# A hybrid diffusion step on one core: the large weight matrices in slabs of one 16 KB run per partition

## The reference, cut to what matters

```
mod = silu(c) @ w_mod[l] + b_mod[l]                 # 1024 x 6144, six blocks of 1024 columns
h   = rms(x, norm1_g) * (1 + sc1) + sh1
u   = h @ w_in[l]                                   # 1024 x 2048, split among four mixers
m   = concat(gqa, pooling, conv, diff attention) @ w_out[l]     # 1024 x 1024
x   = x + g1 * m
h2  = rms(x, norm2_g) * (1 + sc2) + sh2
aff = softmax(h2 @ router_w)                        # 16 experts
gate, idx = top_k(aff.T, 2 * n // 16)               # an expert takes 64 latent and 16 context rows
hid = silu(xe @ wg[e]) * (xe @ wu[e])               # xe = h2[idx], three matrices of 1024 x 1024
x   = x + g2 * scatter_add(idx, hid @ wd[e] * gate)
```

## Time and profile before

| | |
|---|---|
| median of three runs | 2182.03 us |
| profiled execution | 2185.27 us, of which the span of the trace is 2183.4 us |
| mean granted TensorE clock | 0.921 of full speed |
| PE busy | 1843.7 us (84%) |
| PE weight load busy | 1504.9 us (69%) |
| DVE, ACT, POOL busy | 26%, 23%, 17% |
| DMA | 536.37 MB in 145094 packets, mean 246 GB/s |
| ring loads | 228 of 2 MB, by SP's queue (q1) |

### The profile page before, as it was taken

One profiled execution on the slowest core, in us unless ns is written; L12 is line 12 of the kernel. 1 busy time (PEld: TensorE's weight loads), 2 busy tenths in 40 slices (PEclk: granted clock), 3 DMA queues, 4 the chain that ended last, 5 costly groups with the idle time before them and its releaser, 6 DMA issues.

```text
span 2183.4 us, 66044 instructions
## 1 busy us (share of the span) xinstructions
PE 1843.7 (84%) x29563; PEld 1504.9 (69%) x29563; DVE 557.7 (26%) x1095; ACT 506.9 (23%) x1256; POOL 363.2 (17%) x345
## 2 busy tenths in 40 slices
PE   2799998893899998899849999979838998999894
PEld 1455787452898888898725558854538988888883
DVE  0240677234010111101113237742231111011111
ACT  0111554111222121221212125522212212212121
POOL 0130766000000000000002235620000000000001
PEclk8899998995999999999969999979869999999997
DMA  9400300832799999999980040037239999999995
GB/s 349 160 0 8 155 1 1 338 119 105 250 395 387 395 395 391 394 396 393 398 299 13 0 161 2 1 139 263 107 109 370 387 391 398 391 395 395 389 395 192
DMA packets 145094, 536.37 MB, mean 246 GB/s; under 512 B 12259, under 2 KB 15745, under 8 KB 144961
## 3 DMA queue, kind: packets, MB, share of 16 engines
q1 hardware_dynamic: 123056, 481.80, 56.3%
q10 hardware_dynamic: 15616, 31.83, 4.2%
q0 software_dynamic: 6336, 21.63, 4.2%
HBM read 510.82 MB, written 27.03 MB: 246 GB/s over the span
## 4 chain that ended last, share of the span: by engine, by line
PE 53%; DMA 34%; DVE 5%; issue 3%; ACTq 2%; ACT 1%; POOLq 1%; POOL 1%; SPq 0%; DVEq 0%
PE PS L609 17%; DMA ring<-in_exp_w_down 14%; DMA ring<-in_exp_w_up 13%; PE PS L506 6%; PE PS L476 5%; PE PS L445 4%; PE PS L414 4%; PE PS L386 3%; PE PS L387 3%; PE PS L459 3%; ACTq L666 2%; DMA x_rows<-arena 2%; DMA arena<-xn_rows,arena 2%; PE PS L388 2%; DMA ring<-in_w_mod 1%
## 5 line engine op out<-in xcount | busy, mean ns | idle before, releaser
L609 PE MATMUL PS<-arena,ring 128*64 128x80 f32 x24576 | 913.9, 237 | 92.8 <-DMA ring<-in_exp_w_up 39.6
L609 PEld LDWEIGHTS PS<-arena,ring 128*64 128x64 f32 x24576 | 901.1, 140 | 108.2 <-issue 107.8
L880 ACT ACTIVATE arena<-PS,modB,modA 128x64 f32<-128x64 f32 (+1 forms) x544 | 154.0, 419 | 416.7 <-PE PS L597 416.7
L1393 POOL DMA_INDIRECT x_rows<-arena x32 | 45.7, 1429 | 763.8 <-DVE arena L1223 763.8
L506 PE MATMUL PS<-ring,H 128*128 128x512 f32 x320 | 139.2, 593 | 1.7 <-ACTq L653 1.7
L1210 DVE TENSOR_TENSOR arena<-arena,PS 128x320 f32<-128x320 f32 x64 | 31.4, 490 | 329.7 <-PE PS L609 329.7
L506 PEld LDWEIGHTS PS<-ring,H 128*128 128x128 f32 x320 | 60.0, 190 | 73.8 <-issue 71.7
L476 PE MATMUL PS<-arena 128*128 128x64 f32 x816 | 108.7, 274 | 1.6 <-DVE arena L1076 1.5
L445 PE MATMUL PS<-arena,H 128*128 128x512 f32 x192 | 104.4, 625 | 6.5 <-POOL H L1319 5.0
L476 PEld LDWEIGHTS PS<-arena 128*128 128x128 f32 x816 | 105.6, 199 | 2.4 <-DVE arena L1076 1.9
L1062 DVE TENSOR_REDUCE stat<-PS 128x1 f32<-128x640 f32 (+1 forms) x120 | 86.0, 716 | 64.5 <-PE PS L446 57.6
(11 more groups left out here) (193 smaller groups left out, 1681.9 us busy)
## 6 DMA issues: line engine op xcount, KB each, us to landing
ring<-in_exp_w_gate SPq DMA_DIRECT2D x64, 2048.0 KB, 19.1
ring<-in_exp_w_up SPq DMA_DIRECT2D x64, 2048.0 KB, 24.0
ring<-in_exp_w_down SPq DMA_DIRECT2D x64, 2048.0 KB, 17.9
ring<-in_w_mod SPq DMA_DIRECT2D x24, 2048.0 KB, 16.6
ring<-in_w_in SPq DMA_DIRECT2D x8, 2048.0 KB, 22.2
arena<-x_rows ACTq DMA_DIRECT2D x25, 512.0 KB, 6.3
ring<-in_w_out SPq DMA_DIRECT2D x4, 2048.0 KB, 14.8
x_rows<-arena ACTq DMA_DIRECT2D x10, 512.0 KB, 2.6
```

Source lines behind the costliest of these rows:

```text
L609: last = mm(PS[r0:r0 + HD, b0 + j // 4, (j % 4) * CAP:(j % 4 + 1) * CAP], ring[:, 2 * m + k // 4, k % 4, j * P + r0:j * P + r0 + HD], movi ...
L880: last = do(xeT[:, jj, c0:c1], PS[:, 6 + part, j * CAP + c0:j * CAP + c1], ACT.Identity, bias=modB[:, 1, v, jj:jj + 1], scale=modA[:, 1, v ...
```

## The change

kernel() lays out the six large matrices anew before the launch (slabs()). w_mod, w_in and w_out become [layer, column block, half, partition, k, 1024], the expert matrices [layer, expert, half, partition, k, 1024]. The 2 MB of a slot are then one stretch of memory, in which the 16 KB of a partition stand together. slot_load() takes such a slab as it is, without the rearrange, and the callers index column block and half. The bytes of a slot, its place in SBUF and the number and order of loads are the same.

```diff
@@ -266,26 +266,26 @@
 
             def slot_load(l, rnd, s, src):
                 sp.wait_ge(slot_used[s], l * ROUNDS + rnd + CREDIT)
-                sp.dma_start(ring[:, s, :, :], src.rearrange("(k p) n -> p k n", p=P)).then_inc(slot_ready[s], 16)
+                sp.dma_start(ring[:, s, :, :], src).then_inc(slot_ready[s], 16)
 
             with sp.Fori(0, LAYERS) as l:
-                def matrix_load(l, rnd, m, source, c0):
+                def matrix_load(l, rnd, m, source, b):
                     for h in range(2):
-                        slot_load(l, rnd, 2 * m + h, source[l, h * 512:(h + 1) * 512, c0:c0 + D])
+                        slot_load(l, rnd, 2 * m + h, source[l, b, h, :, :, :])
 
                 for b, m, rnd in MOD_SEQ[:2]:
-                    matrix_load(l, rnd, m, ins["w_mod"], b * D)
+                    matrix_load(l, rnd, m, ins["w_mod"], b)
                 matrix_load(l, 0, 2, ins["w_in"], 0)
-                matrix_load(l, 1, 0, ins["w_in"], D)
+                matrix_load(l, 1, 0, ins["w_in"], 1)
 
                 sp.wait_ge(params_loaded, 16 * N_PARAMS * (l + 1))
                 for b, m, rnd in MOD_SEQ[2:]:
-                    matrix_load(l, rnd, m, ins["w_mod"], b * D)
+                    matrix_load(l, rnd, m, ins["w_mod"], b)
                 matrix_load(l, 2, 2, ins["w_out"], 0)
                 with sp.Fori(0, EXPERTS) as e:
                     for m, w in enumerate(("exp_w_gate", "exp_w_up", "exp_w_down")):
                         for h in range(2):
-                            slot_load(l, 3 + e, 2 * m + h, ins[w][l, e, h * 512:(h + 1) * 512, :])
+                            slot_load(l, 3 + e, 2 * m + h, ins[w][l, e, h, :, :, :])
 
 
             sp.wait_ge(phase_done, 4 * LAYERS * PHASES)
@@ -1459,6 +1459,15 @@
          "state_gqa_v": (1, 2, 128, 2, 64), "state_diff_k": (1, 2, 128, 4, 64), "state_diff_v": (1, 2, 128, 4, 64)}
 
 
+def slabs(name, a):
+
+    if name in ("w_mod", "w_in", "w_out"):
+        a = a.reshape(2, 2, 4, 128, a.shape[2] // 1024, 1024).transpose(0, 4, 1, 3, 2, 5)
+    elif name in ("exp_w_gate", "exp_w_up", "exp_w_down"):
+        a = a.reshape(2, 16, 2, 4, 128, 1024).transpose(0, 1, 2, 4, 3, 5)
+    return np.ascontiguousarray(a)
+
+
 def kernel(**inputs):
     import concourse.bacc as _bacc
     from concourse.bass_utils import run_bass_kernel_spmd as _run
@@ -1466,7 +1475,7 @@
     nc = _bacc.Bacc("TRN2", target_bir_lowering=False, num_devices=1)
     arrays, ins, outs = {}, {}, {}
     for name, a in {**inputs, **shape_constants()}.items():
-        a = np.ascontiguousarray(a)
+        a = slabs(name, np.asarray(a))
         arrays[f"in_{name}"] = a
         ins[name] = nc.dram_tensor(f"in_{name}", a.shape, mybir.dt.from_np(a.dtype), kind="ExternalInput").ap()
     for name, shape in _OUTS.items():
```

## The result

The changed kernel takes 2308.95 us (2307.74 to 2309.37, four runs) against 2181.32 us for the kernel before (four runs, one more than at the head): a ratio of 1.0584, interval 1.0566 to 1.0603. It is slower by 128 us; forecast were 76 us and a range up to 2300 us, so the direction and the mechanism held and the size did not. Its profiled execution took 2308.97 us, span 2307.1 us, mean granted clock 0.895.

A forecast was written before the change was run, and what follows sets the result against it. DMA engines were taken to bound the expert loops, with the POOL loop taking over: 30 x (35.7 - 33.27) = +73 us, with 0 + 2 + 2 - 1 elsewhere +76, so 2185.3 + 76 - 3.2 = 2258 us; range 2215 to 2300.

The forecast's parts named there:

- The bound before, and the slack of 3.7 us behind it: Expert loops: DMA engines set the 33.60 us period; the loop through POOL needs 29.9 us, leaving 3.7 us of slack.
- The packet, 0.613 us: Ring loads: a 16 KB packet takes 0.613 us on one engine, against 0.640 for four of 4 KB.
- Turns packet by packet, 2.7 us more for each transfer: POOL's scatter and gather: each of six packets waits 0.453 us longer behind a ring packet, 5.4 us for both transfers.
- the time before the first packet: POOL's loaded transfers: time lost before their first packet stays as it is, assumed to come from bytes in flight.
- I take off 1.2 us for that: Expert loop: the ring idles a little and then does not delay POOL, so 4.2 us are added instead of 5.4.
- That adds 1.6 us on the same loop: Down block after PE's wait: at the lower clock it takes 10.82 instead of 9.19 us, making the period 35.7 us.
- The upper bound of the period, 37 us: Expert period with the ring pending throughout: 29.9 + 5.4 + 1.6 us.
- Outside the expert periods, +3: Phase 1: 0 us in layer 0, +2 in layer 1; scatter closing layer 0: +2; w_mod wait: -1.
- Rival A: Expert loop: ring gains, POOL's transfers are not delayed; period 32.3 us, -29 us, 2152 us in all; chance 0.15.
- C: Expert loop: nothing much, runs cut to 4 KB or loop at 33.3 to 33.8 us; 2180 to 2200 us; chance 0.13.
- Rival B: Ring: a 16 KB packet takes 0.716 us, 37.3 us per expert, +121 us, about 2307 us in all; chance 0.10.
- the signs that were to show the forecast right: Profile: about 35,500 q1 packets, slower landings, gather PE's largest wait, no up or down weight waits, down 10.8 us, DMA share below 1.

## Why the prediction was wrong

Step by step:

- The bound before, and the slack of 3.7 us behind it: right. The run with the earlier gather on 4 KB shows that the loop was hidden.
- The packet, 0.613 us: right, 0.612.
- Turns packet by packet, 2.7 us more for each transfer: right. The scatter lands in 10.2 instead of 7.7 us, the gather in 10.2 instead of 7.1: +2.5 and +3.1, 5.6 together, where 5.4 stood before the deduction. That the time before the first packet stays as it was, an assumption in brackets there, held too.
- "I take off 1.2 us for that": this step failed. The idle time of the ring was to fall into POOL's transfers. It falls elsewhere. The down load's last packets take turns with the scatter's, so that the scatter itself keeps the load from being through (its two halves, issued from 958.10 on, land 7.7 and 13.8 us after their issue, where 10 were taken for the whole); the gate load is issued at 969.00, while the scatter is still under way, and with the up load, issued from 977.74 on, stands against the whole gather; and all loads are done when POOL is silent, during down (share 0.71). Full price was due: 1.4 us per period too little (5.6 - 4.2), 42 us over 30 periods.
- "That adds 1.6 us on the same loop": mis-sized, 1.9 (14.5 instead of 12.65 us from the turn to the end of y). I counted the slow down block and forgot that the turn of the rows before it runs at the low clock too (1.33 instead of 0.77 us), although the place was the right one. 9 us over 30 periods. With the 42 above these make the 51 us between the 2258 us forecast and the 2309 measured; the smaller errors about cancel.
- The upper bound of the period, 37 us, had both at nearly full price and still fell short of 37.6. By it the whole is 30 x (37 - 33.27) + 3 = 115 us more, 2297, and the range ended 3 us above that, with next to nothing left for an error in the other terms.
- Outside the expert periods, +3: right as far as single executions tell. The run with only w_mod, w_in and w_out in slabs is 3 us slower. In the traces of before and after, the part ahead of the first scatter is 2.7 us shorter (forecast 0, between -3 and +5), and from the last scatter of layer 0 to the first of layer 1 it is 3.4 us longer (forecast +2 for layer 1, +2 for the scatter and part of the -1).
- Rival A fell by the landing times, C by the packet count and by the period of 37.6 us. Rival B gave 2307 us, next to the measured time, by a mechanism that isn't there: its packet was to take 0.716 us and PE was to wait for the ring. That its time fits is luck; the waits tell it apart.

All the signs that were to show the forecast right came, two of them larger than forecast: 35,504 packets, the gather as PE's largest wait (6 us instead of 4), no waits for expert weights, 10.2 us for both landings (instead of 9.6 and 9), 10.7 us for down, and a DMA share below 1 in the loop as a whole (0.91 from 600 to 1100 us).

## What to carry to other kernels

A longer run made this stream of bulk loads a few per cent faster (410, 422 and some 430 GB/s alone with 4, 8 and 16 KB) and the small transfers of another queue slower (the gather 7.1, 8.0 and 10.2 us, the scatter 7.7, 8.4 and 10.2), because the two queues gave way to each other packet by packet. So before lengthening runs, look for a chain of small transfers that shares the engines, count its packets, and compare what they will wait with its slack; better, take them off the chain first. And where a stall moves on to the path that sets the end, look at the clock in the instructions right behind it, all of them: here a wait of 6 us cost 2 us more than itself.

## What the runs showed of the hardware beyond that

A loop body that is a little longer can cost far more than its instructions: 72 added products per round, some 5 us of work, raised the instruction queue from 50 to 322 packets and gave PE 12 us per expert of idle time with no one to wait for (382 us over 32). Six wide products with about the same run time (5.4 us) left the queue at 50 packets.
